# Latent norm and context projection: three slots of split weights, the split ahead of the evacuation, the first tap from PSUM

## The reference, cut to what matters

```
h  = rmsnorm(x,   norm_w) * (1.0 + scale[:, None]) + shift[:, None]   # latent, 2048 x 1024
hc = rmsnorm(ctx, norm_w) * (1.0 + scale_c) + shift_c                 # context, 256 x 1024
cols_c = in_projection(hc, w_in, ("m_xbc", "m_dt"))                    # context: 2048 + 32 columns
xbc_c  = silu(depthwise_conv_centred(cols_c["m_xbc"], conv_w, conv_b)) # width 3, three taps
```

## Time and profile before

| | us |
|---|---|
| median of 3 runs | 4275.51 (4273.19 to 4277.01) |
| the profiled execution, its time | 4276.4 |
| its span | 4274.6 |
| PE busy | 3708.5 (87%) |
| DVE busy | 1663.0 (39%) |
| ACT busy | 1162.1 (27%) |
| POOL busy | 915.8 (21%) |
| mean granted clock of TensorE | 0.938 |

### The profile page before, as it was taken

One profiled execution on the slowest core, in us unless ns is written; L12 is line 12 of the kernel. 1 busy time (PEld: TensorE's weight loads), 2 busy tenths in 40 slices (PEclk: granted clock), 3 DMA queues, 4 the chain that ended last, 5 costly groups with the idle time before them and its releaser, 6 DMA issues. The chain is left out here.

```text
span 4274.6 us, 49330 instructions
## 1 busy us (share of the span) xinstructions
PE 3708.5 (87%) x18426; PEld 3067.7 (72%) x18426; DVE 1663.0 (39%) x1979; ACT 1162.1 (27%) x2308; POOL 915.8 (21%) x449
## 2 busy tenths in 40 slices
PE   6599999999999999967989978996456886799879
PEld 2588888888888888846977766764445775699867
DVE  6600443004333400045435443443176765455332
ACT  4311111111011111123764433442103552211022
POOL 0311222112222222110000000000056662433241
PEclk8799999999999999988999999998688998899989
DMA  6411111111111111179995665445785443443343
GB/s 244 154 59 74 70 67 69 74 74 73 64 69 74 74 74 74 54 283 298 293 247 140 146 143 138 114 122 156 256 307 200 155 159 128 148 137 128 110 141 123
DMA packets 595897, 588.97 MB, mean 138 GB/s; under 512 B 285627, under 2 KB 534619, under 8 KB 583387
## 3 DMA queue, kind: packets, MB, share of 16 engines
q1 hardware_dynamic: 515853, 421.13, 33.7%
q10 hardware_dynamic: 79920, 166.22, 10.0%
HBM read 375.84 MB, written 211.42 MB: 137 GB/s over the span
## 5 line engine op out<-in xcount | busy, mean ns | idle before, releaser
L563 PE MATMUL pl_bank<-hl_hi,pl_w_hi 128*128 128x512 f32 x2336 | 923.0, 395 | 17.1 <-POOL pl_w_lo L548 17.1
L564 PE MATMUL pl_bank<-hl_lo,pl_w_hi 128*128 128x512 f32 x2336 | 922.6, 395 | 0.0
L565 PE MATMUL pl_bank<-hl_hi,pl_w_lo 128*128 128x512 f32 x2336 | 922.6, 395 | 0.0
L563 PEld LDWEIGHTS pl_bank<-hl_hi,pl_w_hi 128*128 128x128 f32 x2336 | 440.8, 189 | 120.0 <-issue 17.3
L565 PEld LDWEIGHTS pl_bank<-hl_hi,pl_w_lo 128*128 128x128 f32 x2336 | 440.8, 189 | 103.1
L564 PEld LDWEIGHTS pl_bank<-hl_lo,pl_w_hi 128*128 128x128 f32 x2336 | 440.9, 189 | 102.9
L622 DVE TENSOR_SCALAR pl_acc<-pl_raw,pl_taps 128x2048 f32<-128x2048 f32 x40 | 83.8, 2094 | 930.2 <-ACT pl_raw L587 930.2
L545 POOL TENSOR_TENSOR pl_w_hi<-pl_w,pl_zero 128x1024 fp32r<-128x1024 f32 x73 | 138.3, 1894 | 1246.2 <-PE pl_bank L565 1242.0
L1338 POOL TENSOR_TENSOR st_faded<-st_state,ssd_whole 128x1024 f32<-128x1024 f32 x36 | 82.7, 2306 | 1209.0 <-DVE st_state L1365 1153.0
L1078 DVE TENSOR_TENSOR conv_prod<-conv_bank,conv_spec 128x512 f32<-128x512 f32 x256 | 175.3, 690 | 246.8 <-DMA conv_spec<-spec_s 208.1
L587 ACT ACTIVATE pl_raw<-pl_bank 128x512 f32<-128x512 f32 x160 | 91.7, 598 | 630.5 <-PE pl_bank L565 383.4
(11 more groups left out here) (224 smaller groups left out, 6748.3 us busy)
## 6 DMA issues: line engine op xcount, KB each, us to landing
conv_spec<-spec_s SPq DMA_DIRECT2D x504, 128.0 KB, 2.9
pl_w<-in_w_rec SPq DMA_DIRECT2D x73, 512.0 KB, 3.4
kern_s<-taps_res SPq DMA_DIRECT2D x16, 2048.0 KB, 7.0
spec_xin<-kern_s SPq DMA_DIRECT2D x64, 512.0 KB, 5.4
spec_s<-spec_res ACTq DMA_DIRECT2D x128, 256.0 KB, 3.9
st_xb<-tok_s SPq DMA_DIRECT2D x36, 768.0 KB, 6.9
u_s<-pl_res ACTq DMA_DIRECT2D x24, 1024.0 KB, 3.8
xbc_s<-pl_res ACTq DMA_DIRECT2D x16, 1024.0 KB, 3.8
```

The lines of the kernel that those rows point to most:

```text
L563: pe.matmul(out, w_hi[:, q, m], h_hi[:, k, r], start=(k == 0), stop=False)
L564: pe.matmul(out, w_hi[:, q, m], h_lo[:, k, r], start=False, stop=False)
L565: mm = pe.matmul(out, w_lo[:, q, m], h_hi[:, k, r], start=False, stop=(k == KT - 1))
```

## The change

Four edits, all in `phase_norm`:

1. `w_hi` and `w_lo` get three slots in place of two (`n % 3`); `w`, the weights as loaded, keeps two. `weights(n)` then waits for the matmuls of n-3 in place of n-2.
2. On ACT `weights(n + 2)` moves from behind the evacuation of block n to ahead of the wait for block n's matmuls.
3. The first tap (L451) reads the PSUM bank in place of the copy in `raw`. It still waits for the evacuation. The other two taps read `raw` as before.
4. Since DVE now reads the bank, PE waits before block n for the first tap of block n-2 as well (`s_tap`, which each conv raises twice).

```diff
--- before.py
+++ after.py
@@ -289,7 +289,7 @@
         c_hi, c_lo = ph.sb("c_hi", [P, KT, CTX], F32R), ph.sb("c_lo", [P, KT, CTX], F32R)
         x = ph.sb("x", [P, 4, 2, 512])
         w = ph.sb("w", [P, 2, D])
-        w_hi, w_lo = ph.sb("w_hi", [P, 2, D], F32R), ph.sb("w_lo", [P, 2, D], F32R)
+        w_hi, w_lo = ph.sb("w_hi", [P, 3, D], F32R), ph.sb("w_lo", [P, 3, D], F32R)
         taps = ph.sb("taps", [P, N_CONV * NTAP])
         raw = ph.sb("raw", [P, 2, CTX + 2])
         acc = ph.sb("acc", [P, 2, CTX])
@@ -354,7 +354,7 @@
         def _(pool):
             for n in range(NW):
                 pool.wait_ge(s_whi, n + 1)
-                nc.gpsimd.tensor_tensor(w_lo[:, n % 2, :], w[:, n % 2, :], w_hi[:, n % 2, :].bitcast(F32),
+                nc.gpsimd.tensor_tensor(w_lo[:, n % 3, :], w[:, n % 2, :], w_hi[:, n % 3, :].bitcast(F32),
                                         ALU.subtract).then_inc(s_wlo, 1)
 
         @block.tensor
@@ -364,12 +364,13 @@
                 pe.wait_ge(s_wlo, n + 1)
                 if n >= 2:
                     pe.wait_ge(s_ev, n - 1)
+                    pe.wait_ge(s_tap, 2 * n - 3)
                 out = bank[n % 2][:, 0:CTX]
                 for k in range(KT):
                     m = slice(k * P, (k + 1) * P)
-                    pe.matmul(out, w_hi[:, n % 2, m], c_hi[:, k, :], start=(k == 0), stop=False)
-                    pe.matmul(out, w_hi[:, n % 2, m], c_lo[:, k, :], start=False, stop=False)
-                    mm = pe.matmul(out, w_lo[:, n % 2, m], c_hi[:, k, :], start=False, stop=(k == KT - 1))
+                    pe.matmul(out, w_hi[:, n % 3, m], c_hi[:, k, :], start=(k == 0), stop=False)
+                    pe.matmul(out, w_hi[:, n % 3, m], c_lo[:, k, :], start=False, stop=False)
+                    mm = pe.matmul(out, w_lo[:, n % 3, m], c_hi[:, k, :], start=False, stop=(k == KT - 1))
                 mm.then_inc(s_mm, 1)
 
         def place(n):
@@ -391,9 +392,9 @@
 
             def weights(n):
                 act.wait_ge(s_w[n % 2], 16 * (n // 2 + 1))
-                if n >= 2:
-                    act.wait_ge(s_mm, n - 1)
-                nc.scalar.activation(w_hi[:, n % 2, :], w[:, n % 2, :], ACT.Copy).then_inc(s_whi, 1)
+                if n >= 3:
+                    act.wait_ge(s_mm, n - 2)
+                nc.scalar.activation(w_hi[:, n % 3, :], w[:, n % 2, :], ACT.Copy).then_inc(s_whi, 1)
 
             def finish(n):
                 act.wait_ge(s_conv, n + 1)
@@ -407,6 +408,8 @@
                     weights(n // 2 - 2)
             done = KT
             for n in range(NW):
+                if n + 2 < NW:
+                    weights(n + 2)
                 act.wait_ge(s_mm, n + 1)
                 if n < 2 * KT:
                     if n >= 2:
@@ -415,8 +418,6 @@
                 else:
                     act.wait_ge(s_st[n % 2], 16 * (n // 2))
                     nc.scalar.activation(res[:, n % 2, :], bank[n % 2][:, 0:CTX], ACT.Copy).then_inc(s_ev, 1)
-                if n + 2 < NW:
-                    weights(n + 2)
                 for _ in range(2):
                     if done < 2 * NX:
                         high(done)
@@ -448,7 +449,7 @@
                 dve.wait_ge(s_ev, n + 1)
                 if n >= 2:
                     dve.wait_ge(s_res, n - 1)
-                nc.vector.tensor_scalar(acc[:, q, :], raw[:, q, 1:CTX + 1], w1, bias, ALU.mult, ALU.add).then_inc(s_tap, 1)
+                nc.vector.tensor_scalar(acc[:, q, :], bank[q][:, 0:CTX], w1, bias, ALU.mult, ALU.add).then_inc(s_tap, 1)
                 dve.wait_ge(s_tap, 2 * n + 1)
                 nc.vector.scalar_tensor_tensor(out=acc[:, q, :], in0=raw[:, q, 0:CTX], scalar=w0, in1=acc[:, q, :],
                                                op0=ALU.mult, op1=ALU.add).then_inc(s_tap, 1)
```

## The result

The changed kernel takes 4285.06 us (median of 16 runs, 4277.74 to 4294.88) against 4274.09 before (16 runs, 4267.68 to 4282.6). The ratio is 1.0023, with a 95% interval from 1.0015 to 1.0031: slower by 9.8 us, between 6.4 and 13.2. The forecast was 12.3 slower. The profiled execution took 4286.77 us against 4276.4.

The account below looks back on a forecast made before the run. The ring through ACT, DVE and the load queue was taken to pace the stage. With PE serial, 4.6 + 2.28 = 6.88 us a block, 15 x 6.88 = 103.2, +12.3 us: 4287.8 against the 4275.5 median, range 4281 to 4300.

Parts of the forecast that it names:

- The new wait makes PE serial: On PE: block n waits for a tap that needs block n-1 evacuated, so the two banks no longer overlap; period 6.88 us.
- The hand-over, 2.28: From a block's last matmul through evacuation, `high`, `low` and first tap to the next block: 2.28 us of idle PE.
- The clock falls between blocks and comes back in each: PE's clock drops to half in each gap and recovers within the block, which takes 4.6 us.
- The first two blocks stay: At the stage's start nothing moves: the evacuation of block 1 stays at 101.19.
- The rest is unchanged: What follows the stage's last evacuation stays the same, so the stage's +12.3 us goes into the total.
- No wait for loads of any size: On ACT, the split (L396) would show no wait of any size for its weight loads.
- the slack I had put at 2.1: On ACT: the split and load are ready 2.1 us before PE delivers the block, so loads no longer bound.
- Rival A, a full clock: PE stays at full clock and the loads bound: 5.81 us a block, 4271.7 us, no slower; chance 0.12.
- The loss of some 0.5 at POOL: Under a full clock, the second tap on DVE meets POOL and loses some 0.5 us: 6.05 a block, 4275 us.
- the row at 90.16: A DVE instruction with two tiles in SBUF that took 1.73 us beside POOL, where its like takes 0.5.
- Rival B, no recovery within a block: PE's clock stays at half through each block: 7.6 us a block, +23 us, 4299 us; chance 0.09.
- the block at 149.09: A block on PE before the change: 3.3 us at clock 0.50, then 1.2 at 0.99; taken to show recovery within a block.

Follow-up runs that it names:

- e2: The changed kernel with the first tap reading `raw` again and PE's wait for the tap kept, though it guards nothing; ratio to before 1.0035.
- e6: The changed kernel with the three taps of block n-1 moved ahead of low(8 + 2n) on DVE; ratio to before 0.9985.
- e4: The changed kernel with a third PSUM bank for the projection from block 8 on, so PE waits for block n-3; ratio to before 1.0003.
- e3: The changed kernel with 16 matmuls of no result behind each of blocks 4 to 15, filling PE's idle time; ratio to before 1.0027.
- e9: The changed kernel with the weight load of n+2 ahead of the load of x in SyncE's queue; ratio to before 1.0025.
- e5: The kernel before with edits 3 and 4 alone: first tap from PSUM and PE's wait for it; ratio to before 1.0070.
- e8: The kernel before with edits 1 and 2, SyncE's weight load ahead of the load of x, and taps ahead of the last `low`; ratio to before 0.9957.
- e1: The kernel before with edits 1 and 2 alone: three slots and the split ahead of the evacuation; ratio to before 1.0000.
- e11: The changed kernel with 12 matmuls of no result behind each of blocks 4 to 15; ratio to before 0.9999.

## Why the prediction was right

The direction, the place and the mechanism held, and the experiments show them; the size was 12.3 us against 9.8 measured (6.4 to 13.2). In the time, two errors meet: the stage grew by more than I said, and later phases gave some back. Each is measured on one pair of profiled executions. That the total came so close is in part luck.

- *The new wait makes PE serial.* Shown: the wait alone brings the loss (e2), and moving the tap (e6) or adding a bank (e4) removes it.
- *The hand-over, 2.28.* It is 2.38 in the profile. The evacuation reaches `high` in 0.28 (171.42 to 171.70) where I had 0.37; `low` follows 0.71 later and the tap 0.67, as I had them. The tap is the term I mis-sized, 0.53 long from PSUM for my 0.41, 0.57 to the next for my 0.44. It lay inside my bounds, nearer to the lower one. From the tap's end to PE's first matmul it is 0.15 (173.61 to 173.76) for my 0.05, which no row stood behind.
- *The clock falls between blocks and comes back in each.* Shown by the windows, and as the cause by e3. The block takes 4.45 for my 4.6. The errors of hand-over and block cancel: 6.83 for 6.88, and from block 1 to block 16 103.1 us for 103.2. By e2 the hand-over's part of this isn't chance, since a shorter one made the block longer by as much. The 4.6 I had from blocks behind some 3.6 us of idleness, not 2.4, and the rows of before don't say why it should hold there.
- *The first two blocks stay.* Off by 1.3 us. The evacuation of block 1 came at 102.50 for 101.19: PE began 1.05 later (94.02 for 92.97), and then the split that now stands ahead waited for its load. So the stage grew by 13.5 us for my 12.3 (205.56 for 192.10). In e2 the same place came at 101.34, in e9 at 103.09, so part of this is scatter.
- *The rest is unchanged.* The first matmul of the next phase moved from 204.73 to 218.22, by 13.5, but the span grew by 10.4 only. Three us came back in later phases, which the edit does not touch. The first 1.3 of them came in the next phase, where the clock stood at half for 5.8 us from the first matmul on before and for 3.0 in the changed kernel; by the start of the long convolutions (2228.2 and 2238.6) all three were back. That the stage's loss goes into the total one for one held only to these three us.
- *No wait for loads of any size.* Half right: the split waits 12 times, 10.2 us in all. The first three waits are 4.8, 0.8 and 2.4 us and fall at the start of the stage, where they delay the first evacuations by some tenths; the later ones are 0.2 to 0.4. Behind each of these ACT stands another 1.7 to 2.0 us waiting for PE, which is the slack I had put at 2.1, so they cost nothing (e9).
- *Rival A, a full clock.* Its price was nearly right where e3 forces its condition: 5.93 us per block while the loads bind (8 blocks from 121.80 to 169.27), for my 5.81, and 5.5 in the last four. The loss of some 0.5 at POOL that I added didn't come in e3, whose second taps take 0.63 us at most. That DVE's second tap can inherit the wait at POOL, as the row at 90.16 had it, is shown by e6. The Trainium skill (SBUF — State Buffer, Who interferes with whom) says that a DVE instruction with two SBUF inputs contends with a GpSimd one that reads SBUF, and those rows agree: 2.56 us in place of 0.48.
- *Rival B, no recovery within a block,* did not occur in the changed kernel; in e5, behind 3.33 us, it did in about every other block. The Trainium skill (TensorE: Matmul & The Clock Gate, HAM oscillation) describes a kernel whose every burst starts at half rate behind a wait of 3 to 5 us. The changed kernel's trace agrees, behind 2.38 us, in the milder form of the forecast: 3.3 us at 0.54 and 1.1 at 1.00.

My reading of the rows of before left two blocks out. I took 3.6 us of idleness to mean a start at half clock, and "two more blocks" of 4.4 to 4.6 us to be a recovery like that of the block at 149.09. These two began behind as long a gap, and at the full clock:

```profile
124.73 0.39 PE L370 MATMUL nl_bank<-nl_c_hi,nl_w_hi 128*128 128x256 f32 x1 [3.47 <-POOL nl_w_lo L357]
...
161.42 0.39 PE L370 MATMUL nl_bank<-nl_c_hi,nl_w_hi 128*128 128x256 f32 x1 [3.63 <-POOL nl_w_lo L357]
```

The clock fell inside them, and in windows of them it stood at half:

```profile
126.00:128.00 2.00, 2.00 (x11) 2.00 (x11) 1.90 (x3) 2.00 (x4) 0.27 (x1) 0.50 0.21 70
...
163.00:165.00 2.00, 2.00 (x11) 2.00 (x10) 1.69 (x4) 2.00 (x5) 0.59 (x1) 0.50 0.20 66
```

In the first it came back before the end, in the second it didn't. So the rows of before bore out that a block costs some 4.5 us with the clock part full and part half, but not that it must begin at half.

## What to carry to other kernels

Before an engine is given one more buffer to read, look at what stands ahead of the reading instruction on its own in-order engine: if that needs the writer's next block, two buffers are one. Such a wait shows in no busy time, only in who releases the writer, and one idle gap per block can cost the writer its clock too. Here that was the whole price, measured against a kernel whose loads set 6.06 us a block; beside a faster one (e8, 5.04 us) a serial order with the 5.5 of e3 should cost by itself, which no run tested. And an edit worth nothing by itself (the split moved ahead, worth nothing in e1 and 19 us of the stage between e5 and the change) has to be priced in the order that the other edits make, not in the one of before.

## What the runs showed of the hardware that I had not expected

- With gaps of 2.25 (e2) and 2.38 us (the change) between blocks of some 4.5 us TensorE's clock fell once per block; with gaps of 0.5 to 1.4 us between bursts of 5.0 us (e3) it did not once. The length of a gap didn't decide it alone: a block behind 2.38 us ran at 1.00 throughout (e11 at 118.54), and the fall came up to 1.3 us after a block had begun (before, at 161.42).
- The spacing of the blocks was 6.82 or 6.83 us whether the tap took 0.40 or 0.53: a hand-over longer by 0.13 made the block shorter by as much. A small saving in such a ring showed nothing. e9 came to the same 6.83 from spacings of 7.0 at its start; what sets the figure no run here was made to show.
- A first tap of 256 columns takes 0.53 us from PSUM and 0.40 from SBUF with POOL idle, and 1.29 from SBUF with POOL at work. From PSUM with POOL at work it takes 0.54 (e6).
